# A hybrid decoder step on one core: prelude reordered, the norm beside the last modulation block, decay products moved, one function table set

## The reference

```
mod = silu(c) @ w_ada + b_ada                     # 9 condition rows, 6 x 1024 columns
sh1, sc1, gt1, sh2, sc2, gt2 = split(mod, 6)
h = rms_norm(x, norm_mix_w) * (1 + sc1) + sh1
(dn_qkv, dn_z, dn_a, dn_b, ssm_xbc, ssm_z, ssm_dt, gate_dn, gate_ssm) = split(h @ w_in)
g    = -exp(dn_A_log) * softplus(dn_a + dn_dt_bias);  beta = sigmoid(dn_b)
dt   = softplus(ssm_dt + ssm_dt_bias);                A = -exp(ssm_A_log)
qkv  = silu(causal_conv(dn_qkv)); xbc = silu(causal_conv(ssm_xbc) + bias)
o    = gated_delta(q, k, v, g, beta, state);          y = ssd(xs, dt, B, C, A, state)
mix  = (sigmoid(gate_dn) * dn_out(o) + sigmoid(gate_ssm) * ssm_out(y)) @ w_out
x    = x + gt1 * mix
x    = x + gt2 * moe(rms_norm(x, norm_ffn_w) * (1 + sc2) + sh2)   # top-1 group, top-2 of 8 experts
y    = rms_norm(x, final_norm_w) * (1 + scale_f) + shift_f
```

## Time and profile before

| | |
|---|---|
| three runs | 853.31, 849.39, 851.57 us; median 851.57 |
| profiled execution | 853.74 us, of which the span of the trace is 852.0 |
| TensorE busy | 736.1 us (86%) |
| TensorE weight loads | 534.8 us (63%) |
| VectorE, ScalarE, GpSimd busy | 264.0, 223.6, 97.4 us |
| granted TensorE clock, mean | 0.93 |
| moved by DMA | 195.88 MB, mean 230 GB/s |
| table loads on ScalarE | 33, each 1.28 us; 12 at line 1486, 12 at line 1487 |

### The profile page before, as it was taken

How to read it: one execution, slowest core, us unless ns; L and a number is a source line. 1 busy time by engine, 2 the same in 40 slices (tenths; PEclk the granted TensorE clock), 3 DMA queues, 4 the chain that set the end, 5 groups by cost and what they waited for, 6 DMA issues and landing times.

```text
span 852.0 us, 19975 instructions
## 1 busy us (share of the span) xinstructions
PE 736.1 (86%) x8393; PEld 534.8 (63%) x8394; DVE 264.0 (31%) x737; ACT 223.6 (26%) x523; POOL 97.4 (11%) x229
## 2 busy tenths in 40 slices
PE   2779999999985679999899899983898989989985
PEld 2567777776764457677676677732565656655543
DVE  0035413430135445555561112135111111111132
ACT  1331113123722431252254100151112122121125
POOL 7000000010101330000000000001222222222200
PEclk9769999999996888999999999976899999999996
DMA  7825679998443656315201706874899999999801
GB/s 259 229 96 198 230 261 330 325 327 303 101 115 91 157 150 183 114 51 173 51 26 39 295 0 259 334 295 180 309 411 411 414 413 413 414 412 414 346 14 55
DMA packets 108728, 195.88 MB, mean 230 GB/s; under 512 B 9964, under 2 KB 71097, under 8 KB 100488
## 3 DMA queue, kind: packets, MB, share of 16 engines
q1 hardware_dynamic: 106760, 189.94, 62.2%
q0 software_dynamic: 1920, 5.25, 1.7%
HBM read 185.40 MB, written 9.77 MB: 229 GB/s over the span
## 4 chain that ended last, share of the span: by engine, by line
PE 79%; DVE 7%; ACT 5%; issue 4%; DMA 4%; SPq 1%; DVEq 0%; ACTq 0%; POOLq 0%
PE ps L1110 17%; PE ps L520 10%; PE ps L1268 7%; PE ps L493 5%; PE ps L533 5%; PE ps L438 4%; PE ps L1052 4%; PE ps L417 3%; PE ps L496 3%; PE ps L421 2%; PE ps L483 2%; ACT arena L1496 1%; DMA arena<-in_w_ada 1%; PE ps L527 1%; PE ps L429 1%
## 5 line engine op out<-in xcount | busy, mean ns | idle before, releaser
L1110 PE MATMUL ps<-arena 128*128 128x288 f32 x576 | 144.0, 410 | 0.0
L1110 PEld LDWEIGHTS ps<-arena 128*128 128x128 f32 x576 | 108.9, 191 | 31.1 <-DMA arena<-in_w_in 0.9
L520 PE MATMUL ps<-arena 128*32 128x128 f32 x2432 | 86.5, 278 | 16.0 <-issue 14.0
L520 PEld LDWEIGHTS ps<-arena 128*32 128x32 f32 x2432 | 68.8, 111 | 40.5 <-issue 39.2
L1268 PE MATMUL ps<-arena 128*128 128x288 f32 x256 | 71.8, 425 | 4.1 <-ACT arena L1619 4.1
L1268 PEld LDWEIGHTS ps<-arena 128*128 128x128 f32 x256 | 47.5, 195 | 20.8 <-issue 8.8
L493 PE MATMUL ps<-level,arena 32*128 32x256 f32 x624 | 45.4, 406 | 0.5 <-DVE arena L760 0.5
L533 PE MATMUL ps<-arena,hact 128*32 128x256 f32 x608 | 40.7, 385 | 0.0
L391 POOL DMA_INDIRECT arena<-h_rows,idx_now x38 | 37.5, 987 | 9.5 <-issue 9.5
L755 DVE TENSOR_TENSOR h_row<-h_row,ps 128x64 f32<-128x64 f32 x38 | 8.4, 221 | 97.3 <-ACT h_row L614 97.3
L614 ACT ACTIVATE h_row<-ps 128x64 f32<-128x64 f32 x38 | 8.5, 223 | 111.2 <-PE ps L520 111.2
(11 more groups left out here) (433 smaller groups left out, 1030.7 us busy)
## 6 DMA issues: line engine op xcount, KB each, us to landing
arena<-in_w_exp_gate SPq DMA_DIRECT2D x32, 1024.0 KB
arena<-in_w_exp_up SPq DMA_DIRECT2D x32, 1024.0 KB
arena<-in_w_exp_down SPq DMA_DIRECT2D x32, 1024.0 KB
arena<-in_w_ada SPq DMA_DIRECT2D x12, 2048.0 KB, 10.3
arena<-in_w_in SPq DMA_DIRECT2D x18, 1024.0 KB, 5.7
arena<-in_w_ada_final SPq DMA_DIRECT2D x4, 2048.0 KB, 15.0
arena<-in_w_in SPq DMA_DIRECT2D x16, 512.0 KB
arena<-in_state_ssm_rec SPq DMA_DIRECT2D x8, 512.0 KB, 6.3
```

Of the source, the lines that this page charges most:

```text
L520: l = mm(ps[CW * q:CW * (q + 1), 5, 0:P].rearrange("p (g f) -> p g f", g=2), xwin[:, at:at + CW], gate_up[:, :, k, f:f + HF], start=(k == ...
L1110: l = mm(ps[:, 2 + 2 * sl + m, 0:TOK], w_ring[sl][:, k, m * P:(m + 1) * P], HN[:, k, :], start=(k == 0), stop=(k == KT - 1))
```

## The change

Five things, in the order of the lists:

- SyncE issues the first two rings of `w_in` ahead of the 14 small loads.
- TensorE's prelude is blocks 0 and 1, x transposes, table transposes (now bank 1), block 2, the sum of squares, block 3, the projection. The norm's root and VectorE's eight multiplications stand between modulation blocks 2 and 3.
- Scale and shift of the prompt columns are split: ScalarE does tiles 0 to 3, VectorE tiles 4 to 7.
- The small products leave the place ahead of the projection. They are one product group with `wsm` stationary and 288 columns moving, behind the first half of `project(0, True)` (`small_products`, with 12 state transposes); VectorE copies the 24 rows out, and `small_rows`, behind the second half, transposes the other state and the rows. ScalarE evacuates the first pass ahead of the decay functions.
- Five explicit loads of the table set `natural_log_exp_and_others`: after the first Silu, ahead of the q and k norms, ahead of the decay exponentials, after the Sigmoid of the gates, after the expert loop.

```diff
+            for sl in range(2):
+                load(w_ring[sl], wi[:, :, sl * WN:(sl + 1) * WN], f"win_ld{sl}")
             load(wsm[:, :, 0:4], wi[:, :, C_A:C_A + 4], "small_ld")
...
-            for sl in range(2):
-                load(w_ring[sl], wi[:, :, sl * WN:(sl + 1) * WN], f"win_ld{sl}")
...
+            first_block(0)
+            first_block(1)
+            e.wait_ge(S("x_ld"), 48)
+            for k in range(KT):
...
+                for t, (o, p) in enumerate(TILES):
+                    l = tr(ps[:, k % 4 + 2, o:o + p], x_tok[0:p, t, k * P:(k + 1) * P], ident[0:p, 0:p])
+                l.then_inc(S("x_mm"), 1)
+            e.wait_ge(S("tab_ld"), 16 * 10)
+            tr(ps[:, 1, 0:A_ROWS], tabA, ident[0:A_ROWS, 0:A_ROWS])
+            tr(ps[:, 1, 128:128 + B_ROWS], tabB, ident[0:B_ROWS, 0:B_ROWS]).then_inc(S("first_mm"), 1)
+            first_block(2)
             e.wait_ge(S("sq"), 1)
...
             l.then_inc(S("ms_mm"), 1)
...
+            first_block(3)
...
+            def small_products():
+
+                e.wait_ge(S("small_ld"), 16 * 14)
+                for k in range(KT):
+                    l = mm(ps[0:24, 0, 0:TOK], wsm[:, k, :], HN[:, k, :], start=(k == 0), stop=(k == KT - 1))
+                l.then_inc(S("gsm_mm"), 1)
...
+            def small_rows():
+
+                e.wait_ge(S("gsm_row"), 1)
...
+                e.wait_ge(S("halo_read"), 1)
+                for t, (o, p) in enumerate(TILES):
+                    l = four(t, ps[:, 1, t * 24:(t + 1) * 24], gsm_rows[:, o:o + p], ident[0:24, 0:24])
+                l.then_inc(S("gsm_mm"), 1)
...
-            for t, (o, p) in enumerate(TILES):
-                for k in range(KT):
-                    l = four(t, ps[:, 1, t * 24:(t + 1) * 24], HN[:, k, o:o + p], wsm[:, k, :], start=(k == 0), stop=(k == KT - 1))
-            l.then_inc(S("gsm_mm"), 1)
...
+                    if first:
+                        (small_rows if sl else small_products)()
...
             act(c_tok, c_tok, ACT.Silu).then_inc(S("c_silu"), 1)
+            nc.scalar.preload_act_table_set(LN_EXP)
...
+                if i == 3:
+                    e.wait_ge(S("root"), 1)
+                    for k in range(KT):
+                        l = tt(HN[:, k, :], xT[:, k, :], rstd[:], ALU.mult)
+                    link(l)
                 e.wait_ge(S("ada_mm"), i + 1)
...
-            e.wait_ge(S("root"), 1)
-            modulated(HN)
+            e.nop().then_inc(S("x_scaled"), KT)
+            for k in range(KT // 2, KT):
+                ts(HN[:, k, 0:SEQ], HN[:, k, 0:SEQ], scl[:, k, 0:1], modT[:, SHIFT1 + k, 0:1], ALU.mult, ALU.add).then_inc(S("x_mod"), 1)
             samples_modulated(HN, SHIFT1, 1)
             e.nop().then_inc(S("hn"), 1)
+            e.wait_ge(S("gsm_mm"), 1)
+            v.tensor_copy(gsm_rows, ps[0:24, 0, 0:TOK]).then_inc(S("gsm_row"), 1)
```

More of the change, by code:

```diff
@@ L55 @@
 EPS = 1e-6
+LN_EXP = "natural_log_exp_and_others"
 NEG = -1.0e30
@@ L151, in hybrid_step @@
         HN, _ = carve(HN_AT, KT, TOK)
+        gsm_rows, _ = carve(at, TOK, parts=24)
         sq, q = carve(at, KT, TOK)
@@ L1043, in _ @@
             l.then_inc(S("first_mm"), 1)
-            e.wait_ge(S("tab_ld"), 16 * 10)
-            tr(ps[:, 0, 0:A_ROWS], tabA, ident[0:A_ROWS, 0:A_ROWS])
-            tr(ps[:, 0, 128:128 + B_ROWS], tabB, ident[0:B_ROWS, 0:B_ROWS]).then_inc(S("first_mm"), 1)
             def ada_products(slot, bank):
@@ L1060, in _, with first_block @@
             e.wait_ge(S("cT"), 1)
[L1061 to L1071, removed]
-                    for k in range(KT):
-                        if k >= 4:
-                            e.wait_ge(S("xT"), k - 3)
-                        for t, (o, p) in enumerate(TILES):
-                            l = tr(ps[:, k % 4 + 2, o:o + p], x_tok[0:p, t, k * P:(k + 1) * P], ident[0:p, 0:p])
-                        l.then_inc(S("x_mm"), 1)
+            def first_block(i):
+                sl = i % 2
+                e.wait_ge(S(f"ada_ld{sl}"), i // 2 * 16 + 16)
+                if i >= 2:
+                    e.wait_ge(S("mod_read"), i - 1)
+                ada_products(sl, 6 + sl)
+                e.wait_ge(S("mod_row"), i + 1)
+                ada_transposed(sl, 6 + sl)
+            first_block(0)
+            first_block(1)
+            e.wait_ge(S("x_ld"), 48)
+            for k in range(KT):
+                if k >= 4:
+                    e.wait_ge(S("xT"), k - 3)
+                for t, (o, p) in enumerate(TILES):
[5 more added lines that the diff above has]
+            first_block(2)
             e.wait_ge(S("sq"), 1)
-            e.wait_ge(S("col"), 1)
             for k in range(KT):
@@ L1083, in _ @@
             l.then_inc(S("ms_mm"), 1)
-            e.wait_ge(S("small_ld"), 16 * 14)
-            e.wait_ge(S("xT"), 8)
-            for i, halo in enumerate((dn_halo, ssm_halo)):
+            first_block(3)
[4 more added lines that the diff above has]
+                l.then_inc(S("gsm_mm"), 1)
                 for m in range(NQ):
-                    l = tr(ps[:, 2 + i, m * 24:(m + 1) * 24], halo[:, m * P:(m + 1) * P], ident[0:24, 0:24])
+                    l = tr(ps[:, 1, m * 24:(m + 1) * 24], dn_halo[:, m * P:(m + 1) * P], ident[0:24, 0:24])
                 l.then_inc(S("halo_mm"), 1)
+            def small_rows():
+                e.wait_ge(S("gsm_row"), 1)
+                for m in range(NQ):
+                    l = tr(ps[:, 0, m * 24:(m + 1) * 24], ssm_halo[:, m * P:(m + 1) * P], ident[0:24, 0:24])
+                l.then_inc(S("halo_mm"), 1)
+                e.wait_ge(S("halo_read"), 1)
+                for t, (o, p) in enumerate(TILES):
+                    l = four(t, ps[:, 1, t * 24:(t + 1) * 24], gsm_rows[:, o:o + p], ident[0:24, 0:24])
+                l.then_inc(S("gsm_mm"), 1)
             e.wait_ge(S("hn"), 1)
             e.wait_ge(S("x_mod"), KT)
-            for t, (o, p) in enumerate(TILES):
-                for k in range(KT):
-                    l = four(t, ps[:, 1, t * 24:(t + 1) * 24], HN[:, k, o:o + p], wsm[:, k, :], start=(k == 0), stop=(k == KT - 1))
-            l.then_inc(S("gsm_mm"), 1)
-            e.wait_ge(S("halo_read"), 2)
-            e.wait_ge(S("mod_read"), 4)
             def project(i, first, blocks=1, before=3):
@@ L1492, in prompt_modulated @@
             def prompt_modulated(out, shift, n):
-                for k in range(KT):
+                for k in range(KT // 2 if n == 1 else KT):
                     e.wait_ge(S("x_scaled"), KT * (n - 1) + k + 1)
@@ L1499, in _ @@
             prompt_modulated(HN, SHIFT1, 1)
[L1501 to L1506, removed]
             def evac(i, kind, blocks=1, before=3):
@@ L1544, in cv_sample @@
                     "p (b t) -> p b t", t=STEP)[:, :, 0:NT]
-            e.wait_ge(S("halo_read"), 2)
             evac(0, ("u", 0), 0)
+            e.wait_ge(S("gsm_arg"), 1)
+            act(t1[:], t1[:], ACT.Exp, scale=-1.0).then_inc(S("gsm_f"), 1)
+            act(nbeta[:], gsm[:, :, NG:24], ACT.Exp, scale=-1.0)
+            link(act(alog_row[:], alog_row[:], ACT.Exp))
+            e.wait_ge(S("gsm_arg"), 2)
+            act(t2[:], t2[:], ACT.Ln).then_inc(S("gsm_f"), 1)
             with e.Fori(1, 3) as i:
@@ L1707, in _ @@
             v.tensor_copy(cT[:, :, 0:NC], ps[:, 1, 0:KT * NC].rearrange("p (k c) -> p k c", c=NC)).then_inc(S("cT"), 1)
[L1708 to L1711, removed]
             for i in range(4):
+                if i == 2:
+                    e.wait_ge(S("first_mm"), 2)
+                    v.tensor_copy(colB[:], ps[:, 1, 128:128 + B_ROWS])
+                    link(v.tensor_copy(colA[:], ps[:, 1, 0:A_ROWS]))
+                if i == 3:
[3 more added lines that the diff above has]
+                    link(l)
                 e.wait_ge(S("ada_mm"), i + 1)
@@ L1752, in _ @@
                     l = v.tensor_copy(U[:, NQ * i:NQ * (i + 1), SROW + b * STEP:SROW + b * STEP + HALO],
-                                      ps[:, 2 + i, 0:NQ * 24].rearrange("p (m r) -> p m r", r=24)[:, :, 3 * b:3 * b + 3])
+                                      ps[:, 1 - i, 0:NQ * 24].rearrange("p (m r) -> p m r", r=24)[:, :, 3 * b:3 * b + 3])
                 l.then_inc(S("halo_read"), 1)
-            e.wait_ge(S("gsm_mm"), 1)
+            e.wait_ge(S("gsm_mm"), 2)
             e.wait_ge(S("consts"), 1)
```

## The result

| | before | after |
|---|---|---|
| median | 850.74 us (849.39 to 853.31, 4 runs) | 872.85 us (872.11 to 874.72, 4 runs) |
| ratio to before | | 1.0256, 95% interval 1.0229 to 1.0283 |
| span of the profiled execution | 852.0 us | 870.4 us |
| granted TensorE clock, mean | 0.93 | 0.925 |
| table loads on ScalarE | 33 | 10 |

A forecast was written before the change was run, and what follows sets the result against it. Late modulation weights and the chain ahead of the projection, then TensorE alone, were taken as the bound. Gains of 9.8 us by the second pass and 2.4 from tables made 12.2, from 851.57 to 839.3 us; range 833.5 to 846.

The forecast's parts named there:

- From there the chain is TensorE alone: From the projection on, TensorE alone for nearly 150 us, so any time gained ahead of it reaches the end.
- the 0.03 for slower: Chance given to a slower kernel, from small loads landing after 63.5 us, 20 us later than now.
- x and its transposes: Prelude: x complete at 19.9 us, its transposes 4.35 us on TensorE, done at 24.25.
- Mean square: Prelude, now ahead of block 3: 4.37 us, to 33.8; bounds 3.9 at full clock and 7.8 at half clock.
- Table transposes and block 2: Prelude, after the x transposes: 0.6 us for the tables, then 3.68 us for block 2's products, to 28.6.
- norm, block 3 and modulation: After the mean square: multiplications to 37.9 us, block 3 by 37.5, split modulation to 41.9, projection start at 42.0.
- First pass: Projection's first pass: 15.5 us products, 1.5 clock loss, 6.4 moved small products, 0.1; ends 65.5 instead of 75.3, gain 9.8.
- Function set: ScalarE's table loads fall from 33 to about 10; 2.4 us gained beyond the prelude.
- the prelude's 1.28: Table load in the prelude's norm that goes away, 1.28 us, already counted in the projection start at 42.0.
- The loads stay: Rival: preloads don't keep Ln and Exp table loads away; 2.4 and 1.28 us lost, 843.0 us; chance 0.1.
- The clock eats a part: Rival: slow mean square (7.8 us) and slower clock rise at the projection (1.5 more), 844.2 us; chance 0.12.
- The small loads take the wait's place: Rival: small loads land near 54 us, 3 us too late for the first pass, 842.3 us; chance 0.06, 0.03 slower.

The follow-up runs named there:

- e6: The changed kernel with 48 instructions that do nothing in TensorE's program, 28 at the head and 20 after the transposes of c: 841.64 us, ratio 0.9886.
- e8: The changed kernel with the same 48 do-nothing instructions as e6 but without the five table preloads: 845.41 us, ratio 0.9942 to the kernel before.
- e3: The kernel before with 60 do-nothing instructions at TensorE's head, as a control: 851.53 us, ratio 1.0009.
- e11: The kernel before with 76 do-nothing instructions at TensorE's head: median 877.66 us, four executions from 850.92 to 891.55, no ratio given.
- e2: The kernel before with 117 do-nothing instructions at TensorE's head: 892.33 us, ratio 1.0486.
- e5: The changed kernel with 44 small identity matmuls, all into one quarter of output partitions, where TensorE idles in the prelude: 840.46 us, ratio 0.9864.
- e9: As e5, but the small matmuls go round four quarters and 36 more stand ahead of the projection: 840.17 us, ratio 0.9867.
- e4: The kernel before with only the five table preloads added: 845.92 us, ratio 0.9943.
- e12: As e6, but with the first two w_in loads put back behind the small loads: 840.78 us, ratio 0.9886.
- e10: The changed kernel with expert weight loads cut to 16 of 128 partitions from the eighth expert on: 860.9 us, ratio 1.0139.
- e1: The changed kernel with 139 do-nothing instructions at TensorE's head: 843.48 us, ratio 0.9909 to the kernel before.

## Why the prediction was wrong

**The step that failed** is the one on which the whole sum rests: "From there the chain is TensorE alone [...]: whatever is gained ahead of it passes through." It was argued from what instructions wait for, and the expert loop, 550 us behind the edits and untouched by them, was costed at nothing. The edits changed not only when TensorE's instructions run but how many there are, and so where the loop's code lies: 31.8 us. With the loop back in seven blocks the same change gives 841.64 (e6), 2.3 from the forecast and inside its range. Part of that nearness is luck: of the 8.5 us forecast for everything but the tables e8 shows 4.9 (2.6 to 7.1), and the tables gave 4.9 for 3.7; against its own kernel before, e6 has 9.7 (7.6 to 11.7) of the 12.2. Nothing in the rivals had this mechanism, and the range and the 0.03 for slower were too sure by as much.

The sign of it stood in the profile of before: the row `q8 instruction: 36, 0.59` says that every block was brought just once, so that loops were being held, and the count of instructions would have told that the loop is 6.35 blocks long, so that it lies in seven or in eight of them depending on where it starts. Where the boundaries are, and that eight are too many, only the stops showed. The Trainium skill (Runtime: NRT & Kernel Launch, "Instruction fetch mechanics") gives TensorE 128 KiB of instruction memory, 2048 instructions, filled in blocks of 256, and says that a taken branch to a target outside the current window forces a fetch. The trace agrees on the block (36 packets, 0.59 MB, so 16 KB each) and, by e3, e11 and e2, on eight of them; it disagrees with that page's window of two, since loops of seven blocks went round without a fetch.

**x and its transposes.** x was complete at 20.77, not 19.9. The transposes took 6.63 us instead of 4.35, at a granted clock of 0.55: the row I took them from had TensorE busy for 6 us ahead of it, and now it had stood idle 1.5 us. Together 3.2 late; e5 and e9 show the cause of the second.

**Mean square.** 3.88, the lower bound, not 4.37. Table transposes and block 2 took 0.2 less than put in; norm, block 3 and modulation followed within 0.2 us of the forecast, so the projection started at 44.34 for 42.0.

**First pass.** 24.4 us for the 23.5 put in: the clock took 2.4 instead of 1.5; the small products 3.99 + 0.85 + 0.84 + 0.64 = 6.3 for 6.4. No stall for small loads: the last is issued at 43.3 as thought. The gain up to the second pass is 6.5 us instead of 9.8.

**Function set.** 33 loads became 10. With the prelude's 1.28 that stood inside the 9.8, the forecast gives 3.7 for it alone; e4 has 4.9 (3.0 to 6.6), and that interval holds 3.7.

**The rivals.** "The loads stay": no. "The clock eats a part": yes in the transposes and the first pass, 3.2 us, but not in the mean square where it was put. "The small loads take the wait's place": no; and by e12 the order of these loads didn't matter at all, which the forecast hadn't said.

## What to carry to other kernels

When an edit adds or removes instructions ahead of a long loop, count the loop's instructions and compare the packets of the engine's instruction queue with the size of its program: equal means that the loops are held, more means that a loop is fetched again at every round. A gap of "issue" at the first instructions of each round, of nearly the same length every time and much longer than the 1.5 us of a round that is held, is what it looks like, and shifting the code by some instructions that do nothing tests it in one run. And a gain ahead of the projection need not arrive at the end: e9 was 3.3 us ahead of e6 there, and the two can't be told apart by their times.

## What the runs showed of the hardware

- A loop of 1,625 instructions of TensorE runs from its buffer or is fetched anew in each round, depending on where it starts within a block of 256: 841.6 against 879.8 us for a shift of 24 instructions.
- A round that isn't held stands 10.4 us at its head in two stops, or 12.55 in one, with the weights streaming at some 410 GB/s, and 5.8 with a thin stream (e10); a round that is held stands 1.5. The granted clock falls with it: 0.93 over the loop against 0.99.
- Near the limit the same program does either: 850.92 and 891.55 us (e11).
- 139 instructions of semaphore waits that are met take 13.7 us on TensorE (e1: 18.02 against 4.31), 0.1 us each.
- Matmuls of 32 output partitions that all go into the same quarter take three times as long as when they go round the four: the first 24 of them took 8.1 us in e5 and 2.8 in e9, in the same place and both at a granted clock of 1.00.
